# The v and gate projections of gated linear attention in eight half pieces, six of them between the levels of the recurrences

## The chip, the cores and the metric

The kernel runs on one core of one Trainium2 chip, as one program. Its time is the device time of one execution in microseconds. Three runs of the kernel before gave 1223.24 (median), 1217.55 and 1225.26 us. The profiled execution took 1223.71 us.

## The reference

Two model blocks run over 256 positions of width 1024, in float32. The change lies in the first layer's mixer. One projection of the input gives two branches. The first is gated linear attention (GLA, 4 heads, keys of 64, values of 128):

```
p = x @ w_in
gq, gk, gv, gg, glr = split(p_gla)          # 256, 256, 512, 512, 16 columns
log_a = log_sigmoid(glr @ gate_w2 + gate_b) / 16
S_t = diag(a_t) S_{t-1} + k_t^T v_t,  o_t = q_t S_t
o_a = rms_norm(o_a, norm_g) * silu(gg)
```

The second is an RWKV-7 recurrence of 8 heads, S_t = S_{t-1} diag(w_t) + (S_{t-1} a_t) b_t^T + v_t k_t^T and y_t = S_t r_t, followed by a group norm. Both outputs, side by side, are multiplied by an output matrix ("mix"). Then follow a feed-forward layer, an attention layer (MLA), another feed-forward layer, and a second block.

## The kernel before

Large products are made three times: each float32 operand is split into a rounded half ("hi", float32r) and a rest ("lo"), and `mm3` (lines 406 to 409) adds hi x hi, hi x lo and lo x hi in PSUM. Weights come through a ring of three raw buffers (`RING`, 1 MB each) that the SyncE queue fills; a load waits until the piece three before it is free (`sp_piece`). ScalarE rounds a piece (`act_split`, line 380), VectorE subtracts (`dve_split`, line 391) and by that frees the ring slot. Ahead of the mixer's output matrix two pairs of split buffers take turns in the top 8192 columns of the arena, later three.

Each engine's order of work is written out by hand, in the functions `tensor`, `scalar`, `vector`, `gpsimd` and `sync`; semaphores tie steps by name. PSUM has eight banks that are taken in turn (`Banks.take`); a use waits until the bank's former use is free.

The stages around the change are these. After the RWKV projections come the GLA projections: `glr`, then q and k (`qk`, four blocks of 128 columns), then v and gate (`pe_rows(e, "vg", ...)`): four pieces of 256 input rows by 1024 columns, into four banks, for both row tiles. 96 matmuls of 512 columns come of it. VectorE's `dve_vg` puts `dve_operands` 2 and 3 between the splits; GpSimd's `pool_operands` follows each of these, and `pool_rkm` (line 998) stands behind them. `act_vg` evicts v by a copy and the gate by Silu.

Then `pe_turns` (the bonus product of line 1008, transposes, and the gate's low-rank product), `pe_mats` with `dve_mats` (16 products and their masking, lines 1064 and 1072), and the inverse of unit triangular matrices in seven levels (`pe_inverse`, lines 1120 and 1130).

The recurrences (`pe_recurrences` and its fellows) weave two things. GLA is computed in levels -1 to 7: per level a decay product (line 1308, three levels ahead), an exponential on ScalarE (1320), operands QE on VectorE (1329) and KE on GpSimd (1337), products (1353, 1357), and masks on VectorE (1369). The exponentials have four buffers, `EG`. Between the levels stand the steps of the RWKV chunks, by this table:

```
CHUNK = {-1: [0], 0: [1], 1: [2], 2: [3, 4], 3: [5], 4: [6], 5: [], 6: [], 7: []}
```

Steps 0 to 3 belong to the first chunk, and 4 to 6 to the second: right-hand side (0, 4; lines 1190 and, with the carried state, 1195), solution (1, 5; line 1206), output (2, 6; lines 1215, 1218, and 1221 with the state), carried state (3; lines 1227, 1228). Products with the state have 64 rows by 64 columns. `dve_group_norm(0)` follows level 3. Then comes `pe_mix` (1444, 1446, then transposes and the output matrix).

Of the kernel before, what the change touches and what calls it, by code (L numbers as in the profile page):

```python
# [194 lines left out]
def program(nc, a):  # L195
    ctx = ExitStack()
    with ctx:
# [117 lines left out]
        plan_columns("qk", WIN, 8, [(128 * i, 128) for i in range(4)])  # L315
        plan_rows("vg", WIN, 8, 512, 1024)
        gate = len(pieces)
# [64 lines left out]
        def dve_split(e, through):  # L382
            while done["lo"] <= through:
                i = done["lo"]
                done["lo"] += 1
                if pieces[i][3] is not None:
                    dve_modulation_piece(e, pieces[i][3], i)
                    continue
                hi, lo = split(i)
                e.wait_ge(*at(("hi", i)))  # L390
                e.tensor_tensor(lo, raw(i), hi.bitcast(F32), ALU.subtract).then_inc(  # L391
                    *up("lo", ("lo", i), ("raw free", i)))
# [241 lines left out]
        GLR = carve(256)  # L634
        GV = carve(2, 512)
        GG = carve(2, 512)
        G = carve(2, 512)
# [49 lines left out]

        QE, KE, EG = eight_quarters(PP), eight_quarters(AAB), eight_quarters(ALA)

# [282 lines left out]

        def dve_vg(e):
            for k0 in range(0, 8, 2):
                if k0 in (2, 4):
                    dve_operands(e, k0 // 2 + 1)
                dve_split(e, ahead("vg", k0, k0 < 6))

        def act_vg(e):
            for k0 in range(0, 8, 2):  # L980
                act_split(e, ahead("vg", k0, k0 < 6))
            for t in range(2):
                for j in range(2):
                    use = ("vg", t, j)
                    e.wait_ge(*at(("full", use)))
                    if j == 0:
                        k = e.activation(GV[:, t, :], ps(use), ACT.Copy)
                    else:
                        k = e.activation(GG[:, t, :], ps(use), ACT.Silu)
                    k.then_inc(*up("low", ("v", t, j), ("free", use)))  # L990

# [76 lines left out]
        def dve_mats(e):  # L1068
            for s in range(16):
                use = ("m", s)  # L1070
                e.wait_ge(*at(("full", use)))
                e.tensor_tensor(FOUR[:, :, :, s, :], ps(use).rearrange("p (a b t) -> p a b t", a=2, b=2),  # L1072
                                both.unsqueeze(1).to_broadcast([P, 2, 2, P]), ALU.mult).then_inc(
                    *up("masked", use, ("free", use)))
                if s in (2, 3):
                    t = s - 2
# [104 lines left out]
        def pe_chunk(e, step):  # L1181
# [41 lines left out]
            elif step == 3:  # L1223
                b = bank(e, "s0")
                for i in range(4):
                    sl = slice(128 * i, 128 * i + 128)
                    e.matmul(b[:, sl], KB[:, 0, sl], VT[:, 0, sl], start=True, stop=False)
                    k = e.matmul(b[:, sl], KB[:, 1, sl], RHS.rearrange("p (j i v) -> p i j v", j=2, i=4)[:, i],
                                 start=False, stop=True)
                k.then_inc(*up("chunk", ("full", "s0")))  # L1230
# [81 lines left out]
        def act_gla_decay(e, lv):  # L1312
            e.wait_ge(*at(("full", ("gd", lv))))
            if lv < 4:
                if lv == 0:
                    e.wait_ge(*at(("p done", 6, NG - 1)))
            else:
                e.wait_ge(*at(("ke", lv - 4)))
                e.wait_ge(*at(("qe", lv - 4)))
            e.activation(EG[lv % 4], flat_bank(("gd", lv)), ACT.Exp, scale=-1.0 / 16).then_inc(  # L1320
                *up("levels", ("eg", lv), ("free", ("gd", lv))))

        def dve_gla_operand(e, lv):
            e.wait_ge(*at(("eg", lv)))
            if lv >= 4:
                e.wait_ge(*at(("gla used", lv - 4)))
            elif lv == 0:
                e.wait_ge(*at(("glq", 0)))
            e.tensor_tensor(QE[lv % 4], gq, EG[lv % 4], ALU.mult).then_inc(*up("gla_q", ("qe", lv)))

        def pool_gla_operand(e, lv):
            e.wait_ge(*at(("eg", lv)))
            if lv >= 4:
                e.wait_ge(*at(("gla used", lv - 4)))
            elif lv == 0:
                e.wait_ge(*at(("glq", 2)))
            e.tensor_tensor(KE[lv % 4], gk, EG[lv % 4], ALU.mult).then_inc(*up("gla_k", ("ke", lv)))

# [46 lines left out]

        CHUNK = {-1: [0], 0: [1], 1: [2], 2: [3, 4], 3: [5], 4: [6], 5: [], 6: [], 7: []}

        def pe_recurrences(e):
            pe_gla_decay(e, 0)
            pe_gla_decay(e, 1)  # L1390
            for lv in range(-1, 8):
                for step in CHUNK[lv]:
                    pe_chunk(e, step)
                if lv + 3 < 8:
                    pe_gla_decay(e, lv + 3)
                pe_gla_products(e, lv)

        def act_recurrences(e):
            act_gla_decay(e, 0)
            act_gla_decay(e, 1)  # L1400
            for lv in range(-1, 8):
                for step in CHUNK[lv]:
                    act_chunk(e, step)
                if lv + 3 < 8:
                    act_gla_decay(e, lv + 3)
                if lv == 3:
                    act_group_norm(e, 0)

        def dve_recurrences(e):
# [3 lines left out]
            for lv in range(-1, 8):  # L1413
# [4 lines left out]
                dve_gla_products(e, lv)  # L1418
                if lv == 3:
                    dve_group_norm(e, 0)  # L1420
# [12 lines left out]

        def pe_mix(e):
            for t in range(2):
                b = bank(e, ("oa", t))
                if t == 0:
                    e.wait_ge(*at(("att", 7, 1)))
                    e.wait_ge(*at(("v", 1, 1)))
                for h in range(4):  # L1440
# [917 lines left out]
        def tensor(e):  # L2358
# [8 lines left out]
            pe_columns(e, "qk", 4, XT, xt_step("x0"))  # L2367
            pe_rows(e, "vg", 8, 1024, XT, xt_step("x0"))
            pe_turns(e)
# [18 lines left out]
        def scalar(e):  # L2388
# [10 lines left out]
            act_qk(e)  # L2399
            act_vg(e)  # L2400
            act_turns(e)
# [24 lines left out]
        def vector(e):  # L2426
# [8 lines left out]
            dve_qk(e)  # L2435
            dve_vg(e)
            dve_turns(e)
# [52 lines left out]
        xt_free = {"n0": ("used", place_of["vg", 6]), "n1": ("used", place_of[("gu", 0, 20, 1), 0]),  # L2490
                   "n2": ("used", place_of["mout", 6]), "m0": ("used", place_of[("gu", 1, 20, 1), 0]),
# [40 lines left out]
```

## Time and profile before

| | |
|---|---|
| runs, median (lowest, highest) | 1223.24 us (1217.55, 1225.26) |
| profiled execution | 1223.71 us, span 1221.9 us |
| PE busy | 1108.0 us, 91% |
| VectorE busy | 728.8 us, 60% |
| ScalarE busy | 520.3 us, 43% |
| GpSimd busy | 120.8 us, 10% |
| chain that ended last | PE 82%, DVE 11%, ACT 4% |
| HBM read | 188.39 MB, 158 GB/s over the span |
| mean granted TensorE clock | 0.929 |

Engines are PE (TensorE), DVE (VectorE), ACT (ScalarE), POOL (GpSimd), SP (SyncE). A line of an engine in order of time gives start and duration in us, engine, line of the kernel, operation, output and input with their shapes, the count of merged instructions, and in brackets the idle time before them with what ended it. The end of a matmul is modelled and overlaps the next; the distance of two starts is its price. A matmul of full float32 operands shows as two instructions. The granted clock (PEclk) is a mean of its two levels, 0.5 (1.2 GHz) and 1.0 (2.4 GHz).

### The profile page before, as it was taken

The numbers are of one execution on the slowest core, as the hardware profiler recorded it, in microseconds if no ns is written. First come the engines' busy times: TensorE is split into PE (matmuls) and PEld (weight loads), VectorE is DVE, ScalarE is ACT, GpSimd is POOL, SyncE is SP. The second block draws the span as 40 slices with busy tenths as digits, with TensorE's granted clock in tenths as the row PEclk, the third lists the DMA queues.
The fourth block names the chain that finished last, engine by engine and source line by source line (L and its number), as shares of the span: only waits on it lengthen the run. The fifth ranks groups of instructions, "written<-read, shape, count | busy, mean of one in ns | idle before, by whom it ended". The sixth has DMA issues, their size and how long they took to land.

```text
span 1221.9 us, 16887 instructions
## 1 busy us (share of the span) xinstructions
PE 1108.0 (91%) x7036; PEld 978.4 (80%) x7036; DVE 728.8 (60%) x998; ACT 520.3 (43%) x732; POOL 120.8 (10%) x115
## 2 busy tenths in 40 slices
PE   5989899977999999788889599999969996999997
PEld 5788799866999988667667499998759875999885
DVE  3476684465776675656763666666564555666443
ACT  3452333143444343324763444343255555555331
POOL 0005374112100000400000300000010000000000
PEclk8899999669899999898999699999979997999999
DMA  9335000033787777243781678678534332555540
GB/s 284 104 122 173 34 1 2 1 104 103 252 267 240 244 279 270 87 157 132 113 228 40 205 248 271 219 237 283 192 103 139 104 99 69 175 177 184 197 170 35
DMA packets 112413, 193.67 MB, mean 159 GB/s; under 512 B 4658, under 2 KB 85057, under 8 KB 112210
## 3 DMA queue, kind: packets, MB, share of 16 engines
q1 hardware_dynamic: 108674, 179.66, 44.4%
q0 software_dynamic: 3248, 11.83, 4.3%
q8 instruction: 56, 0.92, 0.3%
q10 hardware_dynamic: 416, 1.11, 0.2%
q14 instruction: 19, 0.16, 0.0%
HBM read 188.39 MB, written 4.19 MB: 158 GB/s over the span
## 4 chain that ended last, share of the span: by engine, by line
PE 82%; DVE 11%; ACT 4%; issue 2%; SPq 1%; DMA 0%; POOL 0%; ACTq 0%; DVEq 0%
PE ps L407 22%; PE ps L408 21%; PE ps L409 21%; PE ps L1886 2%; PE ps L1871 2%; PE ps L1120 2%; DVE XL L540 1%; PE ps L1353 1%; DVE ARR L391 1%; PE ps L1864 1%; PE ps L1130 1%; DVE STAT L557 1%; PE ps L1308 1%; DVE XN L554 1%; DVE AR L1072 1%
## 5 line engine op out<-in xcount | busy, mean ns | idle before, releaser
L391 DVE TENSOR_TENSOR ARR<-ring,ARR 128x2048 fp32r<-128x2048 f32 (+1 forms) x147 | 329.3, 2245 | 222.0 <-ACT ARR L380 221.8
L407 PE MATMUL ps<-XH,ARR 128*128 128x256 f32 x1232 | 354.9, 288 | 26.9 <-DVE ARR L391 13.6
L380 ACT ACTIVATE ARR<-ring 128x2048 fp32r<-128x2048 f32 (+1 forms) x147 | 274.7, 1875 | 214.4 <-PE ps L409 165.9
L408 PE MATMUL ps<-XL,ARR 128*128 128x256 f32 x1232 | 351.6, 285 | 0.0
L409 PE MATMUL ps<-XH,ARR 128*128 128x256 f32 x1232 | 351.4, 285 | 0.0
L407 PEld LDWEIGHTS ps<-XH,ARR 128*128 128x128 f32 x1232 | 238.2, 193 | 32.6 <-issue 28.5
L408 PEld LDWEIGHTS ps<-XL,ARR 128*128 128x128 f32 x1232 | 238.3, 193 | 0.0
L409 PEld LDWEIGHTS ps<-XH,ARR 128*128 128x128 f32 x1232 | 238.0, 193 | 0.0
L407 PE MATMUL ps<-ARR 128*128 128x512 f32 x420 | 170.9, 407 | 9.0 <-DVE ARR L492 5.8
L408 PE MATMUL ps<-ARR 128*128 128x512 f32 x420 | 167.4, 399 | 0.0
L409 PE MATMUL ps<-ARR 128*128 128x512 f32 x420 | 167.4, 399 | 0.0
L407 PEld LDWEIGHTS ps<-ARR 128*128 128x128 f32 x420 | 80.2, 191 | 34.5 <-issue 9.5
L409 PEld LDWEIGHTS ps<-ARR 128*128 128x128 f32 x420 | 80.0, 191 | 19.2
L408 PEld LDWEIGHTS ps<-ARR 128*128 128x128 f32 x420 | 80.3, 191 | 18.4 <-issue 0.5
L407 PE MATMUL ps<-ARR,XH 128*128 128x512 f32 (+1 forms) x128 | 50.7, 396 | 5.9 <-DVE XL L540 4.5
L1531 DVE SCALAR_TENSOR_TENSOR AR<-ring,AR 128x1024 f32<-128x1024 f32 x42 | 53.9, 1282 | 1.1
L408 PE MATMUL ps<-ARR,XH 128*128 128x512 f32 (+1 forms) x128 | 49.8, 389 | 0.0
L409 PE MATMUL ps<-ARR,XL 128*128 128x512 f32 (+1 forms) x128 | 49.7, 388 | 0.0
L1621 ACT ACTIVATE ARR<-XN 128x512 fp32r<-128x512 f32 x22 | 13.9, 632 | 81.0 <-DVE XN L1639 81.0
L470 PE MATMUL ps<-CST,XN 128*128 128x128 f32 x96 | 18.4, 356 | 31.7 <-ACT XN L2089 12.6
L470 PEld LDWEIGHTS ps<-CST,XN 128*128 128x128 f32 x96 | 14.9, 183 | 35.4 <-ACT XN L2089 13.5
L600 POOL TENSOR_TENSOR X<-XN,GB 128x1024 f32<-128x1024 f32 x6 | 14.1, 2343 | 280.4 <-ACT XN L578 280.4
(334 smaller groups left out, 1299.0 us busy)
## 6 DMA issues: line engine op xcount, KB each, us to landing
ring<-in_ffn_w_gate_up_dram SPq DMA_DIRECT2D x44, 1024.0 KB, 5.9
ring<-in_w_dram SPq DMA_DIRECT2D x32, 1024.0 KB, 5.3
ring<-in_w_ada_dram SPq DMA_DIRECT2D x24, 1024.0 KB, 5.3
ring<-in_ffn_w_down_dram SPq DMA_DIRECT2D x22, 1024.0 KB, 5.1
ring<-in_even_w_in_dram SPq DMA_DIRECT2D x13, 1024.0 KB, 5.9
ring<-in_w_in_dram SPq DMA_DIRECT2D x9, 1024.0 KB, 5.3
ring<-in_mla_w_q_b_dram SPq DMA_DIRECT2D x6, 768.0 KB, 4.3
ring<-in_even_w_out_dram SPq DMA_DIRECT2D x4, 1024.0 KB, 4.8
```

Source lines behind the costliest of these rows:

```text
L380: e.activation(split(i)[0], raw(i), ACT.Copy).then_inc(*up("hi", ("hi", i)))
L391: e.tensor_tensor(lo, raw(i), hi.bitcast(F32), ALU.subtract).then_inc(*up("lo", ("lo", i), ("raw free", i)))
L407: e.matmul(out, lhs[0], rhs[0], start=first, stop=False)
L408: e.matmul(out, lhs[0], rhs[1], start=False, stop=False)
L409: return e.matmul(out, lhs[1], rhs[0], start=False, stop=last)
L470: k = e.transpose(ps((tag, c // 2))[:, o:o + P], src[:, t, c * P:(c + 1) * P], ident)
L600: e.tensor_tensor(X[:, t, :], XN[:, t, :], GB[:, 0, :], ALU.mult).then_inc(*up("affine"))
L1120: k = e.matmul(b[:, s * P:s * P + P], ALA[:, 4 * g + s, :], ident if lv == 0 else TI[:, 4 * g + s, :], start=True, stop=True)
L1531: k = e.scalar_tensor_tensor(acc, w[:, c, :], CSL[:, k0 + c:k0 + c + 1], acc, ALU.mult, ALU.add)
L1621: e.activation(hi, u, ACT.Copy).then_inc(*up("silu", ("h first", layer, j)))
L1871: k = e.matmul(b[:, TILE[t]], A.q_of(i, t), A.k_of(i, P * (t + 1)), start=True, stop=True)
L1886: k = e.matmul(ps((A.tag, "o", g))[64 * (h % 2):64 * (h % 2) + 64, o + P * t:o + P * t + P], A.v_of(h, j), px[:, (t + j) * P:(t + j) * P + ...
```

## The change

The v and gate projections are no longer four pieces of 256 rows by 1024 columns but four of 512 rows by 512 columns, v's two first. Each is split and multiplied in two halves of 256 rows: eight halves of 12 matmuls. Halves 0 and 1 stay at the front, where they use the split buffer of the first q/k piece. Halves 2 to 7 are multiplied in levels 0 to 5 of the recurrences, behind the chunk step, and are rounded and subtracted one level earlier. They take turns in two small pairs of buffers; one lies in the gate's own place and in the upper half of `ALA`, so `EG` has two buffers now instead of four. The projections sum in banks 6 and 7, first v, then the gate; everything else from there to the mixer takes turns in six banks. The chunk steps have another order: 3 ahead of 2, and steps 2, 4, 5 and 6 fall on levels 2 to 5. The first group norm follows level 4. The v eviction stands in level 1 and the gate's in level 5.

```diff
-        plan_rows("vg", WIN, 8, 512, 1024)
+        for j in range(2):
+            for k0 in (0, 4):
+                place_of["vg", j, k0] = len(pieces)
+                pieces.append((WIN[k0 * P:k0 * P + 512, 512 + 512 * j:1024 + 512 * j].rearrange("(c p) n -> p c n", p=P),
+                               2048, 4, "vg"))
...
-        QE, KE, EG = eight_quarters(PP), eight_quarters(AAB), eight_quarters(ALA)
+        QE, KE, EG = eight_quarters(PP), eight_quarters(AAB), eight_quarters(ALA)[0:2]
...
+        first = ARENA - 8192 + 4096 * (order[place_of["qk", 0]] % 2)
+        lo_half = place(ee + 1024, 1024, of=ARR)
+        VG_SLOT = [halves(first, 1024), halves(first + 2048, 1024)] + 3 * [
+            halves(mats + 6144, 1024), (place(gg_at, 1024, of=ARR), lo_half)]
...
+        def act_vg_half(e, k):
+            i, x = vg_raw(k)
+            e.wait_ge(*at(("raw", i)))
+            if k == 0:
+                e.wait_ge(*at(("used", place_of["qk", 0])))
+            elif k == 2:
+                e.wait_ge(*at(("vg used", 1)))
+            elif k == 3:
+                e.wait_ge(*at(("p done", 6, NG - 1)))
+            elif k > 3:
+                e.wait_ge(*at(("vg used", k - 2)))
+            e.activation(VG_SLOT[k][0], x, ACT.Copy).then_inc(*up("hi", ("vg hi", k)))
+
+        def dve_vg_half(e, k):
+            i, x = vg_raw(k)
+            hi, lo = VG_SLOT[k]
+            e.wait_ge(*at(("vg hi", k)))
+            e.tensor_tensor(lo, x, hi.bitcast(F32), ALU.subtract).then_inc(
+                *up("lo", ("vg lo", k), *([("raw free", i)] if k % 2 else [])))
+
+        def pe_vg_half(e, k):
+            j, c0 = k // 4, 2 * (k % 4)
+            if c0 == 0:
+                for t in range(2):
+                    bank(e, ("vg", j, t), 6 + t)
+            e.wait_ge(*at(("vg lo", k)))
+            for t in range(2):
+                for c in range(2):
+                    m = mm3(e, ps(("vg", j, t)), cut(XT, ALL, c0 + c, slice(t * P, t * P + P)),
+                            cut(VG_SLOT[k], ALL, slice(512 * c, 512 * c + 512)), c0 + c == 0, c0 + c == 7)
...
+        def pe_vg_early(e):
+            banks.n = 6
+            pe_vg_half(e, 0)
+            pe_vg_half(e, 1)
...
+        def dve_vg_early(e):
+            dve_vg_half(e, 0)
+            dve_operands(e, 2)
+            dve_operands(e, 3)
+            dve_vg_half(e, 1)
...
             elif step == 3:
                 b = bank(e, "s0")
+                e.wait_ge(*at(("solved", 0)))
...
-            if lv < 4:
-                if lv == 0:
-                    e.wait_ge(*at(("p done", 6, NG - 1)))
-            else:
-                e.wait_ge(*at(("ke", lv - 4)))
-                e.wait_ge(*at(("qe", lv - 4)))
-            e.activation(EG[lv % 4], flat_bank(("gd", lv)), ACT.Exp, scale=-1.0 / 16).then_inc(
+            if lv == 0:
+                e.wait_ge(*at(("p done", 6, NG - 1)))
+            elif lv >= 2:
+                e.wait_ge(*at(("ke", lv - 2)))
+                e.wait_ge(*at(("qe", lv - 2)))
+            e.activation(EG[lv % 2], flat_bank(("gd", lv)), ACT.Exp, scale=-1.0 / 16).then_inc(
...
-        CHUNK = {-1: [0], 0: [1], 1: [2], 2: [3, 4], 3: [5], 4: [6], 5: [], 6: [], 7: []}
+        CHUNK = {-1: [0], 0: [1], 1: [3], 2: [2], 3: [4], 4: [5], 5: [6], 6: [], 7: []}
...
                 for step in CHUNK[lv]:
                     pe_chunk(e, step)
+                if 0 <= lv < 6:
+                    pe_vg_half(e, lv + 2)
                 if lv + 3 < 8:
                     pe_gla_decay(e, lv + 3)
                 pe_gla_products(e, lv)
...
                 if lv + 3 < 8:
                     act_gla_decay(e, lv + 3)
-                if lv == 3:
+                if lv < 5:
+                    act_vg_half(e, lv + 3)
+                if lv in (1, 5):
+                    act_vg(e, lv // 4)
+                if lv == 4:
                     act_group_norm(e, 0)
...
                 dve_gla_products(e, lv)
-                if lv == 3:
+                if lv < 5:
+                    dve_vg_half(e, lv + 3)
+                if lv == 4:
                     dve_group_norm(e, 0)
```

## Rows read from the trace of the kernel before

**Rows 1.** The page of the whole execution: its span.

```profile
span 1221.9 us, 16887 instructions
```

**Rows 2.** PE in order of time, 105 to 134 us: start, duration, engine, line, operation.

```profile
105.26 0.40 PE L407 MATMUL ps<-ARR,XH 128*128 128x512 f32 x1
...
127.64 1.85 PE L1008 MATMUL ps<-AR 128*128 128x8 f32 x16
...
133.15 2.96 PE L1064 MATMUL ps<-GB,AR 64*128 64x256 f32 x24
```

**Rows 3.** DVE in order of time, two splits of the front.

```profile
102.22 2.29 DVE L391 TENSOR_TENSOR ARR<-ring,ARR 128x2048 fp32r<-128x2048 f32 x1 [6.77 <-ACT ARR L380]
...
107.90 2.73 DVE L391 TENSOR_TENSOR ARR<-ring,ARR 128x2048 fp32r<-128x2048 f32 x1 [1.31 <-ACT ARR L380]
```

**Rows 4.** ACT in order of time, the front.

```profile
105.46 0.60 ACT L933 ACTIVATE AR<-ps 128x512 f32<-128x512 f32 x1 [3.27 <-PE ps L409]
105.95 1.91 ACT L380 ACTIVATE ARR<-ring 128x2048 fp32r<-128x2048 f32 x1
```

**Rows 5.** POOL in order of time, the front.

```profile
105.37 0.93 POOL L957 TENSOR_TENSOR AR<-AR 128x256 f32<-128x256 f32 x1 [8.04 <-issue]
...
107.85 0.64 POOL L966 TENSOR_TENSOR AR<-AR 128x256 f32<-128x256 f32 x1
...
118.90 2.79 POOL L963 TENSOR_TENSOR GB<-AR 128x256 f32<-128x256 f32 x1
...
122.42 1.84 POOL L998 COPY AR<-VEC 64x1 f32<-64x1 f32 x8
```

**Rows 6.** PE in order of time, the recurrences.

```profile
197.16 1.95 PE L1308 MATMUL ps<-CST,AR 128*128 128x128 f32 x16
...
203.36 2.00 PE L1206 MATMUL ps<-AR 128*128 128x64 f32 x16
...
211.50 1.11 PE L1308 MATMUL ps<-CST,AR 128*128 128x128 f32 x8
...
217.19 0.43 PE L1195 MATMUL ps<-AR,GB 64*128 64x64 f32 x2 [0.80 <-DVE AR L1247]
...
217.92 0.43 PE L1195 MATMUL ps<-AR,GB 64*128 64x64 f32 x2
...
224.60 2.07 PE L1308 MATMUL ps<-CST,AR 128*128 128x128 f32 x8
...
237.54 0.43 PE L1215 MATMUL ps<-AR 128*128 128x64 f32 x2
...
238.49 0.43 PE L1215 MATMUL ps<-AR 128*128 128x64 f32 x2
...
240.40 0.69 PE L1215 MATMUL ps<-AR 128*128 128x64 f32 x2
...
242.06 0.69 PE L1215 MATMUL ps<-AR 128*128 128x64 f32 x2
...
259.20 1.35 PE L1444 MATMUL ps<-AR 128*128 128x128 f32 x10 [1.05 <-DVE AR L1371]
```

**Rows 7.** Stretches of 10 us: busy time by engine, then PEclk, DMA share, GB/s.

```profile
220.00:230.00 10.00, 10.00 (x42) 8.61 (x41) 2.39 (x5) 0.60 (x1) 1.80 (x1) 0.50 0.00 0
230.00:240.00 10.00, 10.00 (x56) 9.34 (x55) 4.56 (x8) 1.88 (x2) 1.80 (x1) 0.65 0.01 2
240.00:250.00 10.00, 10.00 (x39) 8.72 (x39) 3.83 (x7) 1.87 (x4) 0.00 (x0) 0.52 0.00 0
250.00:260.00 10.00, 8.95 (x67) 8.56 (x67) 6.55 (x12) 2.37 (x3) 5.09 (x5) 0.63 0.32 99
```

**Rows 8.** PE in order of time, the mixer's first matmuls.

```profile
269.96 0.77 PE L407 MATMUL ps<-ARR 128*128 128x512 f32 x1 [4.44 <-DVE ARR L492]
...
274.37 0.44 PE L408 MATMUL ps<-ARR 128*128 128x512 f32 x1
```

**Rows 9.** DVE in order of time, the masks of one level.

```profile
203.07 1.56 DVE L1369 COPY_PREDICATED AR<-CST,ps 128x512 f32<-128x512 int32 x2
```

More of the change, by code:

```diff
@@ L385, in dve_split @@
                 done["lo"] += 1
+                if pieces[i][3] == "vg":
+                    continue
                 if pieces[i][3] is not None:
@@ L635, in program @@
         GV = carve(2, 512)
+        gg_at = carve.off
         GG = carve(2, 512)
@@ L971, in dve_qk @@
                 dve_operands(e, i // 2)
[L973 to L981, printed above, removed]
-            for t in range(2):
[L983 to L987, printed above, removed]
-                    else:
-                        k = e.activation(GG[:, t, :], ps(use), ACT.Silu)
-                    k.then_inc(*up("low", ("v", t, j), ("free", use)))
+        first = ARENA - 8192 + 4096 * (order[place_of["qk", 0]] % 2)
@@ new lines, in program, with vg_raw @@
+        lo_half = place(ee + 1024, 1024, of=ARR)
+        VG_SLOT = [halves(first, 1024), halves(first + 2048, 1024)] + 3 * [
+            halves(mats + 6144, 1024), (place(gg_at, 1024, of=ARR), lo_half)]
+        def vg_raw(k):
+            i = place_of["vg", k // 4, k % 4 // 2 * 4]
+            return i, RING[i % NRAW][:, k % 2 * 1024:k % 2 * 1024 + 1024]
+        def act_vg_half(e, k):
[10 more added lines that the diff above has]
+            e.activation(VG_SLOT[k][0], x, ACT.Copy).then_inc(*up("hi", ("vg hi", k)))
@@ new lines, in dve_vg_half @@
+        def dve_vg_half(e, k):
[10 more added lines that the diff above has]
+            e.wait_ge(*at(("vg lo", k)))
+            for t in range(2):
+                for c in range(2):
+                    m = mm3(e, ps(("vg", j, t)), cut(XT, ALL, c0 + c, slice(t * P, t * P + P)),
+                            cut(VG_SLOT[k], ALL, slice(512 * c, 512 * c + 512)), c0 + c == 0, c0 + c == 7)
+                steps = [("full", ("vg", j, t))] if c0 == 6 else []
+                if t:
+                    steps.append(("vg used", k))
+                if steps:
+                    m.then_inc(*up("products", *steps))
@@ new lines, in act_vg @@
+        def act_vg(e, j):
+            for t in range(2):
+                use = ("vg", j, t)
+                e.wait_ge(*at(("full", use) if j == 0 else ("vg used", 7)))
+                if j == 0:
+                    k = e.activation(GV[:, t, :], ps(use), ACT.Copy)
+                else:
+                    k = e.activation(GG[:, t, :], ps(use), ACT.Silu)
+                k.then_inc(*up("low", ("v", t, j), ("free", use)))
+        def pe_vg_early(e):
+            banks.n = 6
+            pe_vg_half(e, 0)
+            pe_vg_half(e, 1)
@@ L992, in pool_rkm, with act_vg_early @@
+        def act_vg_early(e):
+            act_vg_half(e, 0)
+            act_vg_half(e, 1)
+        def dve_vg_early(e):
[3 more added lines that the diff above has]
+            dve_vg_half(e, 1)
         def pool_rkm(e):
@@ L1074, in dve_mats @@
                     *up("masked", use, ("free", use)))
-                if s in (2, 3):
-                    t = s - 2
+                if s in (1, 2):
+                    t = s - 1
                     e.wait_ge(*at(("abs", t)))
@@ L1313, in act_gla_decay @@
             e.wait_ge(*at(("full", ("gd", lv))))
-            if lv < 4:
-                if lv == 0:
-                    e.wait_ge(*at(("p done", 6, NG - 1)))
-            else:
-                e.wait_ge(*at(("ke", lv - 4)))
-                e.wait_ge(*at(("qe", lv - 4)))
-            e.activation(EG[lv % 4], flat_bank(("gd", lv)), ACT.Exp, scale=-1.0 / 16).then_inc(
+            if lv == 0:
[4 more added lines that the diff above has]
+            e.activation(EG[lv % 2], flat_bank(("gd", lv)), ACT.Exp, scale=-1.0 / 16).then_inc(
                 *up("levels", ("eg", lv), ("free", ("gd", lv))))
@@ L1328, in dve_gla_operand @@
                 e.wait_ge(*at(("glq", 0)))
-            e.tensor_tensor(QE[lv % 4], gq, EG[lv % 4], ALU.mult).then_inc(*up("gla_q", ("qe", lv)))
+            e.tensor_tensor(QE[lv % 4], gq, EG[lv % 2], ALU.mult).then_inc(*up("gla_q", ("qe", lv)))
         def pool_gla_operand(e, lv):
@@ L1336, in pool_gla_operand @@
                 e.wait_ge(*at(("glq", 2)))
-            e.tensor_tensor(KE[lv % 4], gk, EG[lv % 4], ALU.mult).then_inc(*up("gla_k", ("ke", lv)))
+            e.tensor_tensor(KE[lv % 4], gk, EG[lv % 2], ALU.mult).then_inc(*up("gla_k", ("ke", lv)))
         def pe_gla_products(e, lv):
@@ L1434, in pe_mix @@
         def pe_mix(e):
+            banks.n = 8
             for t in range(2):
@@ L1438, in pe_mix @@
                     e.wait_ge(*at(("att", 7, 1)))
-                    e.wait_ge(*at(("v", 1, 1)))
+                    e.wait_ge(*at(("v", 1, 0)))
                 for h in range(4):
@@ L2367, in tensor @@
             pe_columns(e, "qk", 4, XT, xt_step("x0"))
-            pe_rows(e, "vg", 8, 1024, XT, xt_step("x0"))
+            pe_vg_early(e)
             pe_turns(e)
@@ L2399, in scalar @@
             act_qk(e)
-            act_vg(e)
+            act_vg_early(e)
             act_turns(e)
@@ L2435, in vector @@
             dve_qk(e)
-            dve_vg(e)
+            dve_vg_early(e)
             dve_turns(e)
@@ L2488, in sync @@
             sp_store(e)
-        xt_free = {"n0": ("used", place_of["vg", 6]), "n1": ("used", place_of[("gu", 0, 20, 1), 0]),
+        xt_free = {"n0": ("vg used", 7), "n1": ("used", place_of[("gu", 0, 20, 1), 0]),
                    "n2": ("used", place_of["mout", 6]), "m0": ("used", place_of[("gu", 1, 20, 1), 0]),
```

## The prediction

> **What bounds the kernel now.** I read the page first, then the busy time by stretches of 10 us, then each engine's instructions in order of time over the two stretches that the change touches. The profiled execution has a span of 1221.9 us [rows 1] and took 1223.71 us with what lies around it, 0.5 us above the median of the three runs, so a difference worked out on this trace may be set against the median as it is. TensorE (PE) is the long engine, and the two stretches behave differently.
>
> The v and gate projections run at the front as one dense block: PE goes from 105.26 to 127.64 us without a gap, 96 matmuls of 512 columns, 0.233 us each, at the full clock; the bonus product follows at once and the masks' products start at 133.15 [rows 2]. VectorE (DVE) has slack there (6.77 and 1.31 us idle ahead of two splits) [rows 3], ScalarE (ACT) as well [rows 4]. GpSimd (POOL) ends its own work at 124.3 us, 3.4 us before PE comes to it [rows 5].
>
> The recurrences run from 197.16 to 259.20 us [rows 6]. PE hardly waits there (0.80 us ahead of chunk step 4, 1.05 us at the end), but its granted clock is 0.50, 0.65, 0.52 and 0.63 in the four stretches from 220 to 260 us [rows 7]. With levels of 0.5 and 1.0 these means say 10.0, 7.0, 9.6 and 7.4 us at the lower level (1.2 GHz), 34 us in all. The same work is slower there: the decay product takes 2.07 us against 1.11, and one head of chunk step 6 goes from 0.95 us (237.54 to 238.49) to 1.66 us (240.40 to 242.06) [rows 6]. The clock fell while PE was busy: once in chunk step 4, once in step 6. These two alternate products of 64 rows by 64 columns with others. Chunk step 2 without such products (from 207.87 us) ran at the full clock.
>
> **The front.** 72 of the 96 matmuls leave it, 72 x 0.233 = 16.8 us of PE. That isn't the gain, since something else becomes late. The last q/k product ends at 105.3 us and ACT evicts it until 105.95 [rows 4]. The new order has DVE subtract half 0 ahead of its operands 2 and 3. ACT rounds half 0 in about 1.0 us (half of 1.91, [rows 4]), to 106.95; DVE subtracts it in 1.15 us (half of 2.29, [rows 3]), to 108.2. PE, idle for 2.9 us, multiplies it in 12 x 0.233 = 2.8 us. DVE's two operands take 2.1 us each (between the splits of 102.22 and 107.90, [rows 3]), to 112.4, and half 1 comes to 113.7; PE ends at 116.5 at the full clock. POOL's operand 2 can start about 1 us into DVE's, at 109. One takes 3.1 us undisturbed (105.37 to 108.49), and one with a DVE split beside it has a single instruction of 2.79 us in place of 0.7 [rows 5]. So POOL ends operand 3 at 115.2 to 116.4, and the eight copies behind it, with their memset, add 2.0: 117.2 to 118.4 us. POOL sets the start of the bonus product, at 118 us instead of 127.64: 9.6 us earlier.
>
> Against it stands the clock. The block had none of these gaps, and after a gap of 4.44 us the next dense block began at the lower level [rows 8]. PE now has gaps of 2.9, 2.8 and 1.5 us with 2.8 us of work between. If the clock is low at the bonus product, the 5.5 us up to the masks' products [rows 2] grow by up to 4.8 (the decay product's ratio of 1.86), and the masks' products some more. Nothing in the trace excludes that, or that it doesn't happen. I take half of it, 2.5 us: **front -7 us, between -10 and -3.** The masks and the inverse that follow shift rigidly: with six PSUM banks a mask product waits for the sixth before it rather than the eighth, while DVE is the slower side of that pair; in the inverse each bank comes free by a step that the next product waits for anyway. Both at nothing; if a bank did bind, each of the 16 masks could add a fraction of its 0.6 us.
>
> **The recurrences.** Six halves come in, 6 x 12 x 0.233 = 16.8 us at the full clock. At the lower level a matmul takes 0.44 us (10 of them from 269.96 to 274.37, [rows 8]), or 31.7 us for all. DVE gets six subtractions of 1.15 us and ACT six roundings of 1.0 us; PE's 62 us cover both. Three halves follow a short chunk step (1.8 us, the 2.00 of 203.36 in [rows 6] less its overlap with the next), while their subtraction stands behind two masks of 1.56 us together [rows 9]: 1.56 + 1.15 - 1.8 is 0.9, and the first mask starts before PE has ended the level; I take 0.6 us each, **+1.8 us** (between 0 and the whole 2.7 each, 8). The wait of 0.80 us for the carried state goes away, since step 3 now comes a level earlier. Two buffers of exponentials instead of four make ACT wait for POOL's product two levels back; operands are made three levels ahead, so at nothing. The v piece's ring slots are held until level 4, so the mixer's weights load later, the third of them still three levels ahead of the mixer. The POOL queue keeps its order; its gate product now waits for the last half, two levels ahead of its reader.
>
> Now the clock. What today's lower level costs is 34 us x (1 - 1/1.7) = 14 us, with 1.7 between the ratios 1.75 and 1.86 of the rows and that of chunk step 4, whose ends are less plain. Were the clock full throughout, the stage would take 62.0 - 14 - 0.8 + 16.8 + 1.8 = 65.8 us, **+3.8**. But steps 4 and 6 stay whole: at the full clock 8 x 0.73 = 5.8 us (217.19 to 217.92 for one head, [rows 6]) and 8 x 0.95 = 7.6 us. Both were where the clock fell; a half behind each helps only afterwards. Dense products brought the clock back after 4.4 us at 269.96 [rows 8]. Each fall then costs a part of the step and most of the 4.4 us that follow: low for some 5 to 12 us instead of 17, at 0.43 us lost per us, 2 to 5 us each. I take 3.3 each, **+6.5**. The stage: **+10 us, between +8 and +14.**
>
> On this a rule of the Trainium skill speaks otherwise. The rows show a clock that fell at a PE without idle time, and stayed low for 34 us. The page "TensorE: Matmul & The Clock Gate", section "Why this matters for your kernels", advises keeping TensorE continuously busy and free of long idle gaps so that the clock stays up. Read so, recurrences without gaps would run at the full clock, and the stage after would be the second case below; but the rows from 220 to 260 us already contradict it, so the kind of work matters.
>
> **The sum:** -7 + 10 = +3, on 1223.7: **1227 us**, between -10 + 8 = -2 and -3 + 14 = +11, 1222 to 1235.
>
> **The rivals.**
> Second, the halves keep the clock up through steps 4 and 6. For it: 16.8 us more of PE work, all of it dense, and the state that step 4 needs no longer makes PE wait just before the fall. Against it: the second fall came in step 6 with no wait at all. Then +3.8 - 7 = -3, or -6 with the front's full 10 us: 1214 to 1221, likeliest 1219.
> Third, slower than before: the clock falls in step 4 and the halves, 2.8 us long, don't hold PE dense for long enough to bring it back, being cut by decay products, levels' products and the short waits. Its place is level 3 to level 5. From the fall on, the two remaining halves plus the one behind step 6 run at 0.44: 36 x 0.21 = 7.5 us more, and steps 5, 6 and the levels between stay low as today (14). 16.8 + 1.8 + 7.5 - 0.8 is +25, less 7 to 10 for the front: 1239 to 1242. It decides from the point where the half behind step 4 ends at 0.44 a matmul. Against it: at 237.54 us the clock was up again, after nothing denser than a decay and a level's products [rows 6].
> Fourth, the front gives little: the clock falls in its gaps and stays low through the masks' products, or DVE or POOL is later than worked out. -2 + 10 = +8: 1232. That half 0 stands ahead of DVE's operands speaks for it.
> That the change doesn't do what it says can be left out: the order is written out by hand on each engine.
>
> **Chances.** Forecast 0.58, second 0.22, third 0.11, fourth 0.09. This kernel's runs can tell about 1%, 12 us, from no change. Under 1211 us only the second with an overlooked gain comes, 0.05. Over 1235.5 come the third and a tail of the forecast and the fourth, 0.14. The rest, 0.81, lies within. The range 1213 to 1238 takes in the second and fourth and leaves out most of the third.
>
> **What would show it.** In the trace after: the bonus product at 118 us (at 124 or later the front step is wrong), PE gaps of 2 to 3 us ahead of halves 0 and 1, and POOL's copies as its releaser. In the recurrences 72 matmuls of 512 columns; their mean distance near 0.233 speaks for the second, 0.27 to 0.33 for the forecast, over 0.38 for the third. Start of decay 0 to the last level product: 70 to 75 us expected, 65 in the second, over 80 in the third. Waits ahead of halves 2, 3 and 6 of about 0.6 us, on DVE. The prediction would be wrong as a whole if the mixer after the recurrences changed its length by more than 3 us, which I take as unchanged.

## The result

In 20 runs each the changed kernel took 1229.12 us (median; 1227.51 to 1230.4) and the kernel before 1223.38 us (1215.3 to 1226.52). The ratio is 1.0055, with a 95% interval of 1.004 to 1.007 (the ratios given here lie near those of the means; the two medians give 1.0047). The changed kernel is slower by 5.7 us in the median, a small difference, 2 us above the forecast of 1227 and inside its likeliest case (1222 to 1235). The profiled execution took 1229.39 us, its span is 1227.5 against 1221.9 [rows 1].

The kernel before scatters over 11 us, the changed one over 3.

### The profile page after: what moved, and what is told of

Same layout as the page of the kernel before. It is cut to its first block, busy times and chain, and to the rows that moved or that the text cites. A ratio compares the mean times of both kernels' runs of the same rounds, so it can differ in the third digit from the quotient of the medians.

```text
span 1227.5 us, 16897 instructions
## 1 busy us (share of the span) xinstructions
PE 1106.6 (90%) x7036; PEld 975.1 (79%) x7036; DVE 730.4 (60%) x1002; ACT 517.3 (42%) x734; POOL 118.0 (10%) x115
## 3 DMA queue, kind: packets, MB, share of 16 engines
q0 software_dynamic: 3248, 11.83, 4.3%
## 4 chain that ended last, share of the span: by engine, by line
PE 80%; DVE 11%; ACT 4%; issue 3%; SPq 1%; DMA 0%; POOL 0%; ACTq 0%; DVEq 0%
PE ps L413 22%; PE ps L414 21%; PE ps L415 21%; PE ps L1955 2%; PE ps L1940 2%; PE ps L1180 2%; DVE XL L546 1%; DVE ARR L397 1%; PE ps L1933 1%; PE ps L1190 1%; DVE STAT L563 1%; ACT ARR L384 1%; DVE XN L560 1%; PE ps L476 1%; DVE AR L1132 1%
## 5 line engine op out<-in xcount | busy, mean ns | idle before, releaser
L397 DVE TENSOR_TENSOR ARR<-ring,ARR 128x2048 fp32r<-128x2048 f32 (+1 forms) x143 | 319.5, 2240 | 214.8 <-ACT ARR L384 214.5
L384 ACT ACTIVATE ARR<-ring 128x2048 fp32r<-128x2048 f32 (+1 forms) x143 | 267.0, 1873 | 209.9 <-PE ps L415 160.6
L413 PE MATMUL ps<-ARR,XH 128*128 128x512 f32 (+1 forms) x128 | 54.0, 422 | 13.9 <-DVE ARR L1008 8.1
L414 PE MATMUL ps<-ARR,XH 128*128 128x512 f32 (+1 forms) x128 | 51.8, 404 | 0.0
L413 PEld LDWEIGHTS ps<-ARR,XH 128*128 128x128 f32 x128 | 26.4, 206 | 21.7 <-issue 8.6
```

What stands on the lines that cost most here:

```text
L384: e.activation(split(i)[0], raw(i), ACT.Copy).then_inc(*up("hi", ("hi", i)))
L413: e.matmul(out, lhs[0], rhs[0], start=first, stop=False)
L414: e.matmul(out, lhs[0], rhs[1], start=False, stop=False)
```

## The profile after

TensorE (PE) in order of time over the front, where [rows 2] show the kernel before:

```profile
108.20 0.48 PE L413 MATMUL ps<-ARR,XH 128*128 128x512 f32 x1 [2.98 <-DVE ARR L1008]
...
110.85 0.39 PE L415 MATMUL ps<-ARR,XL 128*128 128x512 f32 x1
115.12 0.80 PE L413 MATMUL ps<-ARR,XH 128*128 128x512 f32 x1 [3.88 <-DVE ARR L1008]
...
119.98 0.63 PE L415 MATMUL ps<-ARR,XL 128*128 128x512 f32 x1
120.40 1.95 PE L1068 MATMUL ps<-AR 128*128 128x8 f32 x16
```

VectorE (DVE) in the same stretch, for [rows 3]:

```profile
106.83 1.22 DVE L1008 TENSOR_TENSOR ARR<-ring,ARR 128x1024 fp32r<-128x1024 f32 x1 [8.26 <-ACT ARR L1002]
...
113.32 1.74 DVE L1008 TENSOR_TENSOR ARR<-ring,ARR 128x1024 fp32r<-128x1024 f32 x1
```

GpSimd (POOL) there, for [rows 5]:

```profile
113.94 1.71 POOL L970 TENSOR_TENSOR GB<-AR 128x256 f32<-128x256 f32 x1
...
116.38 1.84 POOL L1058 COPY AR<-VEC 64x1 f32<-64x1 f32 x8
```

The bonus product starts at 120.40 us, 7.24 us earlier. PE waited 2.98 us for half 0 and 3.88 us for half 1. Half 1 ran at 0.43 us a matmul: the clock was at its lower level there. It was at the full one again during the bonus product (mean clock 0.95 from 120.40 to 122.40 us). POOL was done at 118.2 us and set nothing in this execution. DVE's subtraction of half 1 took 1.74 us where that of half 0 took 1.22, beside a POOL instruction that took 1.71 us instead of 0.78.

The recurrences of the changed kernel on PE, for [rows 6]:

```profile
190.13 1.95 PE L1369 MATMUL ps<-CST,AR 128*128 128x128 f32 x16
...
198.77 0.50 PE L413 MATMUL ps<-ARR,XH 128*128 128x512 f32 x1 [0.44 <-DVE ARR L1008]
...
229.96 0.79 PE L413 MATMUL ps<-ARR,XH 128*128 128x512 f32 x1
...
233.41 0.39 PE L415 MATMUL ps<-ARR,XL 128*128 128x512 f32 x1
...
239.38 0.50 PE L413 MATMUL ps<-ARR,XH 128*128 128x512 f32 x1 [0.44 <-DVE ARR L1008]
...
250.82 0.69 PE L1275 MATMUL ps<-AR 128*128 128x64 f32 x2
...
254.14 0.79 PE L413 MATMUL ps<-ARR,XH 128*128 128x512 f32 x1
...
257.23 0.39 PE L414 MATMUL ps<-ARR,XH 128*128 128x512 f32 x1
...
261.12 0.61 PE L1417 MATMUL ps<-AR 64*128 64x128 f32 x5
263.63 2.17 PE L1513 MATMUL ps<-AR 128*128 128x128 f32 x10 [1.90 <-DVE AR L1431]
...
275.46 0.77 PE L413 MATMUL ps<-ARR 128*128 128x512 f32 x1 [5.50 <-DVE ARR L498]
```

And its stretches of 10 us, for [rows 7] (busy time by engine, then PEclk, DMA share, GB/s):

```profile
220.00:230.00 10.00, 10.00 (x49) 8.20 (x47) 3.60 (x5) 1.32 (x2) 1.81 (x1) 0.65 0.30 105
230.00:240.00 10.00, 9.56 (x56) 8.21 (x56) 4.21 (x6) 1.54 (x2) 1.81 (x1) 0.84 0.00 0
240.00:250.00 10.00, 10.00 (x68) 8.63 (x67) 5.75 (x9) 2.83 (x3) 1.81 (x1) 1.00 0.17 41
250.00:260.00 10.00, 10.00 (x48) 8.24 (x48) 2.88 (x6) 3.64 (x7) 0.75 (x1) 0.66 0.16 65
260.00:270.00 10.00, 7.37 (x57) 6.73 (x53) 8.33 (x15) 2.99 (x3) 2.58 (x4) 0.83 0.35 107
```

Decay 0 starts 7.03 us earlier than before. From there to the mixer's first product pass 73.50 us (190.13 to 263.63) instead of 62.04. The means say 7.0, 3.2, 0 and 6.8 us at the lower level from 220 to 260, 17.0 us against 34. The two falls are in chunk step 4 and chunk step 6 again. Each time the half behind the step started at 0.43 us a matmul (229.96 and 254.14) and ended at 0.23: in this execution the clock came back within it. Three halves waited 0.39 to 0.44 us for DVE.

From the mixer's first product to its output matrix it takes 11.83 us (263.63 to 275.46) instead of 10.76. The sum of the three parts is -7.03 + 11.46 + 1.07 = +5.5 us, and the span grew by 5.6.

## The experiments

All ratios are to the kernel before, in runs on the same chip; the changed kernel's 1.0055 is the level to compare with. The first four kernels ran on another chip than the last four; the kernel before took 1223.81 and 1223.44 us beside them (medians), so a difference in us to the changed kernel's 1229.12 can be set beside the ratios. The intervals are 0.4 to 0.7% wide, which is wide beside some of the effects, so the traces carry the details. A trace shows one execution each, and it need not be a typical one.

**Dense products inside steps 4 and 6.** In the recurrences:

```diff
+            def woven(n):
+                if step in (4, 6) and n in WEAVE:
+                    pe_vg_half(e, 5 if step == 4 else 7, (WEAVE.index(n),))
...
+                        woven(4 * j + i)
...
+        WEAVE = [2, 3, 5, 6]
...
-                if 0 <= lv < 6:
+                if 0 <= lv < 6 and lv not in (3, 5):
                     pe_vg_half(e, lv + 2)
```

`woven` multiplies, after a head, one group of three matmuls of half 5 (in step 4) or of half 7 (in step 6).

> Halves 5 and 7 are no longer behind chunk steps 4 and 6 but inside them, one group of three matmuls of 512 columns after heads 2, 3, 5 and 6. Nothing else changes. Theory A (the clock falls because each of these steps is a long stretch of small products; 17 us at the lower level there, 7.3 us lost): with dense products between the heads the clock stays up for most of both steps, time 5 to 7 us under the changed kernel, 1222 to 1224 us, ratio to the kernel before 0.999 to 1.001. Theory B (it is the products of 64 rows by 64 columns with the carried state that bring the clock down, whatever stands between): the clock falls as now, time as the changed kernel, 1228 to 1230 us, ratio 1.005.

Measured: 1226.1 us (12 runs), ratio 1.002 (0.9993 to 1.0048). The runs fall into two groups, four from 1218.6 to 1221.0 us at a mean clock of 0.941 to 0.945 and eight from 1225.7 to 1230.5 us at 0.930 to 0.938. The profiled run is of the second:

```profile
220.00:230.00 10.00, 9.82 (x60) 8.14 (x58) 3.60 (x5) 1.34 (x2) 1.81 (x1) 1.00 0.31 105
...
240.00:250.00 10.00, 10.00 (x49) 8.38 (x47) 8.21 (x13) 2.79 (x4) 1.76 (x1) 0.67 0.30 105
250.00:260.00 10.00, 10.00 (x47) 8.84 (x48) 1.01 (x2) 2.66 (x4) 0.32 (x1) 0.50 0.00 0
```

Step 4 (221.3 to 230.1 us) kept the full clock. Step 6 lost it in this run at 243.3 us, in its third head, and the four dense groups that followed inside the step ran at the lower clock without bringing it back. From decay 0 to the mixer's first product it took 72.9 us instead of 73.5: what step 4 gained, step 6 lost. Theory A put the gain at 5 to 7 us; the eight runs of the upper group gained less (at most 3.4 us) and the four of the lower one more (8.1 to 10.5). That the clock held in step 6 in those four fits their times, but this kernel has no trace of it. Theory B is out for step 4, whose products with the state are all still there; for step 6 this kernel doesn't decide.

**VectorE's operands ahead of half 0.**

```diff
         def dve_vg_early(e):
-            dve_vg_half(e, 0)
             dve_operands(e, 2)
             dve_operands(e, 3)
+            dve_vg_half(e, 0)
             dve_vg_half(e, 1)
```

> VectorE makes operands 2 and 3 ahead of half 0 instead of between halves 0 and 1. It stands idle from 98.6 to 106.8 us now, so they cost nothing there. Theory A (GpSimd's chain behind the operands, and the gap ahead of half 1, set the start of the bonus product, 120.4 us now): GpSimd ends at 109 us, halves 0 and 1 follow each other from 108.2 us, the bonus product starts at 114, time 6 to 7 us under the changed kernel, 1222 to 1223 us, ratio 0.999 to 1.000. Theory B (the clock or the stages behind it take the gain back): under 3 us, 1226 us or more, ratio 1.002 or more.

Measured: 1223.41 us (12 runs), ratio 1.0006 (0.9983 to 1.0029), 5.7 us under the changed kernel. PE over the front:

```profile
106.70 0.76 PE L413 MATMUL ps<-ARR,XH 128*128 128x512 f32 x1 [4.24 <-DVE ARR L1008]
...
113.67 1.85 PE L1068 MATMUL ps<-AR 128*128 128x8 f32 x16
```

The bonus product starts at 113.67 us, 6.7 us earlier, as theory A said. The ratio is just above what it allowed (0.999 to 1.000), and theory B's 1.002 lies within the interval; the trace decides for A. The recurrences gave a part back: decay 0 starts 7.0 us earlier than in the changed kernel, the output matrix of the mixer 5.7 us. From decay 0 to the mixer's first product it took 75.2 us instead of 73.5, with the same work and waits: the clock was low for 20.8 us of it instead of 17.0, and the halves behind steps 4 and 6 stayed at the lower level almost to their ends (4.9 and 5.2 us, where the changed kernel took 4.4 and 4.3). This run, of 1219.17 us, was the fastest of its twelve.

**Both edits.**

> Both edits together. Theory A for both: the gains add up, 11 to 14 us under the changed kernel, 1215 to 1218 us, ratio 0.993 to 0.996, faster than both kernels. Theory B for either: 1222 us or more.

Measured: 1215.82 us (12 runs), ratio 0.9955 (0.9927 to 0.9982). Eight of the runs lie from 1213.1 to 1215.9 us, four from 1221.1 to 1226.6 at a clock of 0.936 and less. That is theory A: 13.3 us under the changed kernel in the median. It is more than the two medians alone add up to (3.0 and 5.7), since here two thirds of the runs are in the lower group and in the woven kernel one third. The profiled run, of 1215.88 us, is of the lower group and shows what the woven kernel's trace didn't, the clock held in step 6 (234.3 to 244.5 us) as well:

```profile
220.00:230.00 10.00, 9.56 (x65) 8.29 (x65) 4.21 (x6) 1.54 (x2) 1.81 (x1) 1.00 0.15 62
230.00:240.00 10.00, 10.00 (x67) 8.62 (x65) 6.02 (x9) 3.10 (x5) 1.80 (x1) 1.00 0.21 64
240.00:250.00 10.00, 8.11 (x73) 7.24 (x73) 6.43 (x12) 4.34 (x7) 2.85 (x4) 1.00 0.10 43
```

It rules theory B out for step 6 too. The same order of work held the clock in one run and lost it in the other.

**Without the products with the carried state.**

```diff
-                                     start=True, stop=t == 0)
-                        if t:
...
-                            k = e.matmul(b[:, sl], CAR[r, i, t, 0, :], S0[r, i, :], start=False, stop=True)
+                                     start=True, stop=True)
...
-                            k = e.matmul(b[:, sl], CAR[r, i, t, 1, :], S0[r, i, :], start=False, stop=True)
```

> The products with the carried state (64 rows by 64 columns, 8 in chunk step 4, 8 in step 6) are left out, so the second chunk is computed without the first one's state. They take 8 x 0.37 + 8 x 0.37 = 5.9 us of TensorE at the full clock. Theory A or B: without them steps 4 and 6 are shaped like steps 0 and 2, at which the clock stayed up, so it doesn't fall there: 5.9 us of work and 7.3 us of lost clock go, 13 us, about 1216 us, ratio 0.994. Rival (the clock falls in any long stretch of 64-column products): only the work goes, at the mixed clock 7 to 8 us, 1221 to 1222 us, ratio 0.998 to 0.999.

This kernel computes the second chunk without the first one's state. Measured: 1213.23 us (8 runs), ratio 0.992 (0.9892 to 0.9948), 15.9 us under the changed kernel; expected were 13, and 7 to 8 by the rival. Its stretches:

```profile
210.00:220.00 10.00, 10.00 (x79) 9.10 (x79) 3.32 (x5) 3.97 (x8) 1.82 (x2) 1.00 0.06 23
220.00:230.00 10.00, 9.56 (x75) 8.57 (x73) 5.82 (x10) 2.41 (x3) 3.61 (x2) 1.00 0.28 105
230.00:240.00 10.00, 9.56 (x72) 8.64 (x72) 5.75 (x10) 2.83 (x3) 1.81 (x1) 1.00 0.01 2
240.00:250.00 10.00, 7.78 (x68) 6.84 (x68) 9.08 (x16) 4.50 (x7) 3.33 (x4) 1.00 0.48 140
```

The clock never fell in them, so the rival's number is out. But the edit shortens the steps as well: at the full clock step 4 goes from 5.8 to 1.8 us and step 6 from 7.6 to 3.6, 8 us in all where 5.9 were put down. Steps with the state products bring the clock down where nothing dense stands between, and short steps without them don't; whether it is the kind of product or the length of the stretch isn't shown. No kernel here has 64-column products of 128 rows that run on for more than 3.6 us.

**The old order of the chunk steps.**

```diff
-        CHUNK = {-1: [0], 0: [1], 1: [3], 2: [2], 3: [4], 4: [5], 5: [6], 6: [], 7: []}
+        CHUNK = {-1: [0], 0: [1], 1: [2], 2: [3, 4], 3: [5], 4: [6], 5: [], 6: [], 7: []}
```

> The changed kernel with the chunk steps in the order and at the levels of the kernel before (step 2 at level 1, steps 3 and 4 at level 2, 5 at 3, 6 at 4); the halves stay at their levels. Theory (what counts is the two steps with the carried state and the half behind each; the new order only hides the wait for the state, 0.8 us): within 3 us of the changed kernel, 1227 to 1232 us, ratio 1.003 to 1.007. Rival (the new order is what costs or saves): outside of that.

Measured: 1234.44 us (6 runs), ratio 1.0088 (1.0059 to 1.0118), 5.3 us over the changed kernel: the theory misses, the rival holds. PE at the two places where it waits longer:

```profile
260.00 0.49 PE L413 MATMUL ps<-ARR,XH 128*128 128x512 f32 x1 [2.36 <-DVE ARR L1008]
...
269.54 2.47 PE L1513 MATMUL ps<-AR 128*128 128x128 f32 x10 [3.32 <-DVE AR L1431]
```

With no chunk step on level 5, half 7 stands directly behind level 4's products on PE while its subtraction stands behind that level's masks on DVE: a wait of 2.36 us that step 6 covers in the changed kernel. The group norm follows on DVE, and the last levels' masks behind it, so the mixer's first product waits 3.32 us instead of 1.90. The wait for the carried state came back as well, with 1.01 us. The clock had a part too. Its stretches:

```profile
210.00:220.00 10.00, 8.99 (x59) 7.79 (x58) 4.37 (x7) 2.52 (x4) 1.80 (x1) 0.88 0.01 2
220.00:230.00 10.00, 10.00 (x41) 8.13 (x42) 0.78 (x2) 0.99 (x2) 0.31 (x1) 0.60 0.00 0
230.00:240.00 10.00, 9.56 (x70) 8.37 (x67) 5.76 (x9) 2.10 (x3) 3.29 (x2) 1.00 0.31 107
240.00:250.00 10.00, 10.00 (x41) 8.53 (x41) 0.84 (x1) 0.77 (x2) 0.00 (x0) 0.58 0.00 0
250.00:260.00 10.00, 7.64 (x37) 6.27 (x35) 3.23 (x5) 2.83 (x3) 1.80 (x1) 0.74 0.00 0
```

These are 2.4, 8.0, 0, 8.4 and 5.2 us at the lower level, 24 us against 17. Both halves behind the steps with the state ran at 0.44 us a matmul to their ends here (222.61 to 227.90 and 249.39 to 254.68 us), so a half doesn't always bring the clock back while it runs. From decay 0 to the mixer's first product it took 80.8 us instead of 73.5. Of these 7.3 us the waits account for 4.4 (7.56 in all against 3.17); the rest, 3 us, is what 7 us at the lower level cost at 0.43. From there to the output matrix it took 0.9 us more, and what lies ahead of decay 0 and behind that point 1.4 us less each than in the changed kernel's trace; together the spans differ by 5.4 us.

**No half behind steps 4 and 6.**

```diff
-                if 0 <= lv < 6:
-                    pe_vg_half(e, lv + 2)
+                for k in {0: [2], 1: [3], 2: [4, 5], 4: [6, 7]}.get(lv, []):
+                    pe_vg_half(e, k)
```

> Halves 4 and 5 both stand behind step 2 in level 2, and halves 6 and 7 behind step 5 in level 4: no dense products behind steps 4 and 6. The work is the same. Theory (the half behind each step is what shortens the low clock, from 17 us to 10 and 7): the clock stays low for about 17 us after each fall as in the kernel before, 4 to 7 us more, 1233 to 1236 us, ratio 1.008 to 1.011. Rival (the clock comes back by the decay and level products just as soon): 1228 to 1231 us, ratio 1.004 to 1.006.

Measured: 1229.56 us (12 runs; 1224.81 to 1235.87), ratio 1.0063 (1.0039 to 1.0087). By the median the rival is right. The profiled run, of 1234.2 us, is the second slowest. Its recurrences show what the theory described:

```profile
230.00:240.00 10.00, 10.00 (x44) 8.60 (x42) 2.28 (x4) 2.49 (x3) 1.80 (x1) 0.54 0.00 0
240.00:250.00 10.00, 10.00 (x36) 8.60 (x36) 3.66 (x4) 0.00 (x0) 0.00 (x0) 0.60 0.30 107
250.00:260.00 10.00, 10.00 (x65) 8.70 (x64) 6.45 (x11) 2.45 (x4) 1.80 (x1) 0.91 0.00 0
260.00:270.00 10.00, 9.07 (x56) 8.44 (x57) 4.59 (x9) 4.04 (x5) 3.33 (x4) 0.58 0.02 7
```

That is 9.2, 8.0, 1.8 and 8.4 us at the lower level, 27 us against 17. From decay 0 to the mixer's first product it took 76.2 us instead of 73.5 (at 0.43, 10 us at the lower level cost 4.4; the waits are 1.4 us shorter). The span is longer by 4.8 us, but more than half of that isn't the edit's: decay 0 starts 3.4 us later, at 193.57 us, though nothing ahead of it was changed. In other runs less seems to have been lost. What the halves behind the steps are worth over many runs stays open; that the clock can come back within them is seen in the trace of the changed kernel.

**Halves 4 and 6 spread through the steps, 5 and 7 behind them.** The woven kernel with WEAVE = [0, 2, 4, 6], halves 4 and 6 in place of 5 and 7, none on levels 2 and 4 otherwise, and the operands first.

> Operands first as before, and now half 4 lies inside step 4 and half 6 inside step 6, a group of three matmuls behind heads 0, 2, 4 and 6; halves 5 and 7 stay behind these steps. Theory (a step falls only where its small products run on for some us; in the kernel with halves 5 and 7 inside the steps three heads came ahead of the first dense group, and some executions lost the clock in step 6 with no half behind it): no execution falls, the times lose their upper group, median 1213 to 1216 us, all within 5 us, ratio 0.992 to 0.994. Rival (the fall in some executions has nothing to do with where the dense products lie): two groups as there, median 1216 to 1222 us.

Measured: 1216.01 us (12 runs; 1212.62 to 1219.67), ratio 0.9938 (0.9917 to 0.9958). None of the twelve runs lies above 1220 us, where four did with both edits; the scatter is 7 us where at most 5 were expected, and the median, at the edge of the theory, is no lower than that of both edits (1215.82). In the profiled run the clock was full from 190 to 250 us:

```profile
230.00:240.00 10.00, 10.00 (x68) 8.64 (x67) 8.66 (x15) 3.40 (x5) 1.79 (x1) 1.00 0.31 107
240.00:250.00 10.00, 9.19 (x70) 7.74 (x69) 3.26 (x5) 4.04 (x5) 3.29 (x4) 1.00 0.00 0
250.00:260.00 10.00, 5.65 (x32) 5.20 (x32) 8.68 (x14) 4.83 (x5) 0.04 (x1) 0.79 0.34 106
```

**The same, with halves 0 and 1 ready earlier.**

```diff
                 act_split(e, ahead("qk", i))
+                if i:
+                    act_vg_early(e)
...
             act_qk(e)
-            act_vg_early(e)
...
             dve_operands(e, 2)
+            dve_vg_half(e, 0)
+            dve_vg_half(e, 1)
             dve_operands(e, 3)
-            dve_vg_half(e, 0)
-            dve_vg_half(e, 1)
...
+            pool_rkm(e)
+            e.wait_ge(*now("pool_op"))
             for i in range(4):
                 pool_operands(e, i)
-            pool_rkm(e)
```

> As the kernel before it, and ScalarE rounds halves 0 and 1 ahead of its eviction of the last q/k product, VectorE subtracts both between operands 2 and 3, and GpSimd's eight copies go ahead of its operands. TensorE then has no gap of 3 us ahead of half 0; it ends half 1 at 110.7 us instead of 113.8 to 114.1, GpSimd at 109 to 110. Theory (TensorE's own work now sets the front's end): 3 us less than the spread kernel, 1210 to 1213 us, ratio 0.989 to 0.992. Rival (GpSimd or the eviction becomes late instead): less than 1 us gained.

Measured: 1212.17 us (6 runs; 1211.54 to 1214.75), ratio 0.9915 (0.9882 to 0.9947). It is faster than both kernels, by 11 us than the one before (1223.44 beside it) and by 17 than the changed one. PE over the front:

```profile
105.53 0.47 PE L413 MATMUL ps<-ARR,XH 128*128 128x512 f32 x1 [0.73 <-ACT AR L942]
...
111.21 1.84 PE L1075 MATMUL ps<-AR 128*128 128x8 f32 x16
```

The gap ahead of half 0 is 0.73 us, and half 1 ends as the bonus product starts, at 111.21 us; 110.7 was expected. GpSimd is done at 109.3 us, as expected.

## Why the prediction was right

**The front: -7 predicted, -7.03 measured at decay 0.** The sum held and two of its steps did not, so it held in part by luck. "POOL sets the start of the bonus product, at 118 us" failed in this execution: PE set it, 2.2 us after POOL was done (118.2 us, within the 117.2 to 118.4 of the prediction). Half 1 came at 115.12 instead of 113.7 us, because its subtraction took 1.74 us and not 1.15 (DVE and POOL slowed each other, which I had allowed for on POOL only), and after its gap it ran at the lower clock, 5.3 us instead of 2.8. "If the clock is low at the bonus product" didn't come about, since half 1 took the low stretch itself and 120.40 to the masks' products at 126.01 took 5.6 us, against 5.5 before. The 2.5 us put down for the clock (half of 4.8) met 2.5 of it in another place, by chance.

The experiments that left this front alone show how much of it is chance: in the profiled runs without the state products and with no half behind steps 4 and 6 the low clock fell on half 0, half 1 ran at the full one, and POOL did set the start, as forecast:

```profile
118.88 1.92 PE L1068 MATMUL ps<-AR 128*128 128x8 f32 x16 [0.19 <-POOL AR L1058]
119.08 1.92 PE L1068 MATMUL ps<-AR 128*128 128x8 f32 x16 [0.22 <-POOL AR L1058]
```

In the second of them the clock then fell behind the bonus product, and the way to the masks' products took 8.3 us instead of 5.5, the loss that the prediction had described. Decay 0 starts at 190.15, 189.78, 188.70 and 193.57 us in those four kernels (woven, no state, old steps, no half behind), 3.6 to 8.5 us earlier than before; the 7.03 is one draw among these. That VectorE's order was at fault, named under the fourth rival, is shown by the kernel with the operands first: the bonus product starts 6.7 us earlier, and the median is 5.7 us lower.

**Masks and inverse at nothing.** Bonus product to decay 0: 69.52 us before, 69.73 after, as predicted.

**The recurrences: +10 predicted, between +8 and +14; measured +11.5.** Decay 0 to the last level product took 71 us (190.13 to 261.12), 70 to 75 expected. Term by term: 72 matmuls' work of 16.8 us; waits for DVE 1.27 us (1.8 predicted); the wait of 0.80 us gone, but 0.85 us more at the end (1.90 against 1.05), which I had not seen. Without clock losses that makes 62.0 - 14 + 16.8 + 1.3 - 0.8 + 0.9 = 66.2; 73.5 were measured, so 7.3 us were lost to the clock (6.5 predicted) over 17.0 us at the lower level. This sum without losses can be checked: the profiled runs that kept the full clock through the same work took 65.8 us (both edits) and 65.5 us (the two spread kernels) over this stretch, where the prediction put 65.8. The mean distance of the 72 matmuls is 0.28 us (four halves at 0.24, the two behind the steps at 0.36), inside the 0.27 to 0.33 that was to speak for this case. The 0.43 us lost per us at the lower level, read from the rows of before, fits: 7.3 to 7.7 us over 17.0.

**The mixer: unchanged predicted, +1.07 measured.** Its first products came behind the longer wait and ran at the lower clock again (the mean clock from 260 to 270 us is 0.83; the first group took 1.96 us, and 1.19 before). They release the split buffers for ScalarE's roundings, which before had been waiting for the group norm only. I had called this part unchanged, with 3 us as its limit.

**The rivals.** The second (full clock through steps 4 and 6) didn't happen in this kernel, and the kernel with both edits and the spread ones show that it could be had: with dense products inside the steps, not only behind them. Its time range was wrongly worked out: -3 to -6 on 1223.7 gives 1218 to 1221, and nothing leads to the 1214 at its lower end. The third (the halves too short to bring the clock back, so that it stays low to the end) is out for this kernel: the clock came back while both ran. It was a near thing: in the kernel with the old order of steps both halves stayed low to their ends, and the clock came back right behind them. The rule of the Trainium skill that the prediction weighed (page "TensorE: Matmul & The Clock Gate", section "Why this matters for your kernels"), to keep TensorE busy without long idle gaps so that the clock stays up, wasn't enough here either: PE was busy without a gap from 240 to 260 us, with a mean clock of 0.66 in the second half.

**What the prediction had no sight of** is how much the order of the steps is worth: 5.3 us in the median, by covering two waits for VectorE (3.8 us together in the traces) and one for the carried state, and with some 3 us of clock that may differ from one execution to the next. I had counted it as the 0.80 us of the carried state. The sum was right all the same, since its waits were worked out for the new order.

## What to carry to other kernels

Work moved out of a dense stage earns what is late next there, so look at once at the queue order of the engine that feeds the remainder: VectorE stood idle for 8 us and then made GpSimd's operands behind half 0. Dense products put behind a stretch of small ones arrive when the clock is already down; put between them from the first head on, they kept it up in both profiled runs, for the same work, and from the third head on in both for step 4 and in one of two for step 6. And a subtraction that an engine makes for its neighbour wants a long step ahead of its use: the halves behind a short chunk step cost 0.4 us of waiting each, and half 7 none behind step 6 and 2.4 us with no step ahead of it. Last, one trace is one draw: kernels with the same front reached the recurrences at times that lie 4.9 us apart.

## What had not been expected of the hardware

The clock fell with PE busy all the time, in the two steps that alternate products of 64 rows by 64 columns with others. Left out, these products took the fall with them (clock 1.00 from 210 to 250 us), but they took 4 us of each step's length with them too, so their kind and the length are not told apart. With one dense group of three matmuls (0.7 us) behind every second head the clock stayed at 1.00 in the profiled runs of both spread kernels.

How long the clock is low differs from one execution to the next of the same kernel: the woven kernel's runs of 1218.6 to 1221.0 us had a mean clock of 0.941 to 0.945, those of 1225.7 to 1230.5 us 0.930 to 0.938. The scatter of the kernel before, 11 us, goes the same way: beside the experiments its runs under 1219 us had a mean clock of 0.938 to 0.942, those over 1223 us 0.927 to 0.933. Where in it the clock differs isn't shown, since no trace here shows two of its executions side by side.
